# The S5 layer and the last feed-forward pass of a two-layer streaming encoder, computed in token halves and woven into dense passes

## The chip, the cores and the metric

The kernel runs on 1 core of one Trainium2 chip. The metric is the device time of one execution in microseconds (us), lower is better. Three runs of the kernel before stand beside one profiled execution, from which every row below is read.

## The reference

The model has two layers and works on 1024 prompt tokens and 64 sample tokens at once (T = 1088), D_MODEL = 1024, hidden width 2816. All tensors are float32. Layer 0 (a projection, stick-breaking attention beside a gated mixer, an output projection) and its SwiGLU feed-forward are the same before and after. Layer 1 is an S5 state-space mixer, a GLU and a SwiGLU feed-forward; the part that matters is, cut:

```python
def swiglu(h, w_gate, w_up, w_down):
    return (jax.nn.silu(h @ w_gate) * (h @ w_up)) @ w_down

def s5_mixer(h, h0_re, h0_im, ...):
    x_re = einsum('gpc,blgc->blgp', bb_re, ug)         # 64 groups of 16 channels, 64 complex states each
    x_im = einsum('gpc,blgc->blgp', bb_im, ug)
    ...                                                # first step also takes in the given state
    _, _, s_re, s_im = associative_scan(s[t] = a * s[t-1] + x[t])
    y = einsum('gcp,blgp->blgc', c_re, s_re) - einsum('gcp,blgp->blgc', c_im, s_im) + d_skip * u
    gl = gelu(y) @ w_glu
    ga, gb = split(gl, 2)
    return ga * sigmoid(gb), s_re[:, -1], s_im[:, -1]
```

Every layer is x = x + mixer(rmsnorm(x)), x = x + swiglu(rmsnorm(x)); a last rmsnorm follows.

## The kernel before, in words

**Dense matmuls.** Float32 products are made from three fp32r matmuls: every weight slab of 128 x 1024 is split into whi and wlo (slab_hi on ACT, slab_lo on POOL), every activation tile likewise into a high and a low part, and `three` (lines 248 to 253) issues wh*rh, wh*rl, wl*rh into one PSUM accumulation. All of these have a weight tile of 128 x 128.

**Stages.** (1) The input projection in three token chunks (384, 384, 320), with the tables of the S5 layer made beside it. (2) The "mid" stage: attention, output projection and feed-forward of layer 0, in two token halves (512 and 576 tokens, the second in two chunks of 288). It is planned in Python as a list of slots; each slot has dense groups (one PSUM bank each, three banks in turn) and, in some, attention steps, norm tiles or squares. Each engine walks through the same list. Attention of the second half is done beside the feed-forward of the first. (3) S5 (`s5_sp`, `s5_pe`, `s5_act`, `s5_dve`, `s5_pool`), for eight feature tiles f one after the other, over all 1088 tokens as 136 blocks of 8 steps. (4) The GLU (`glu_pe`) and (5) the norm and the feed-forward of layer 1 (`ffn_pe`, a loop of 10 passes and two halves around it), in the three token chunks 384, 384, 320. (6) The last norm, transposes and stores (`out_pe`).

**S5 in detail.** For each f TensorE does: 8 transposes of B (line 1830), 16 matmuls for a 16-row kernel table kt (line 1838, weight tiles 64 x 16), 16 input matmuls x (line 1850, weight tiles 128 x 64, two side by side), then 24 output matmuls y: 8 with the Toeplitz table tm (line 1868, weight tiles 128 x 128) and 16 with the state (line 1870, weight tiles 64 x 128). They are plain float32, and each such matmul stands in the trace as two records. Between x and y VectorE rotates, scans and rotates back (lines 1932 to 1984); the reordering of u, tm and y between partitions goes through DRAM by DMAs that SyncE issues. TensorE issues one f's x, then the y of the f before.

**Order.** Each engine works its own instructions in the written order and waits on semaphores; a wait holds up all that is behind it on that engine. The S5 stage begins when both halves of layer 0 are done, and the GLU needs gelu(y) of all eight f.

## Time and profile before

| | |
|---|---|
| median of 3 runs | 2809.38 us (2804.43 to 2810.51) |
| profiled execution | 2812.7 us, span 2810.9 us |
| mean granted TensorE clock | 0.941 |
| PE busy | 2565.4 us (91%) |
| DVE, ACT, POOL busy | 1166.2, 881.3, 1104.3 us |

The span runs from the first to the last instruction. Engines: PE is TensorE's matmuls, PEld its weight loads, DVE is VectorE, ACT ScalarE, POOL GpSimd, SP SyncE. A granted clock of 1.0 is TensorE's 2.4 GHz, 0.5 its 1.2 GHz. A record's duration overlaps with its neighbours', so the pace of TensorE is read from the distance of two starts, not from durations.

### The profile page before, as it was taken

The page shows a single profiled execution, that of the slowest core. Times are in us where ns is not written, and L with a number is a line of the kernel's source. Part 1 is how long each engine was busy: PE and PEld are TensorE (multiplying, and loading weights), DVE is VectorE, ACT ScalarE, POOL GpSimd, SP SyncE. Part 2 cuts the span into 40 slices and gives each one's busy share as a digit, 9 for nine tenths or more (in the row PEclk, how much of TensorE's full clock was granted, in tenths as well). Part 3 has the DMA queues.
Part 4 walks back from the last instruction along what each step waited for, and adds up shares of the span by engine and source line. Part 5 has one row for each costly group of instructions (what it writes and reads, how often), then busy time and mean ns, then how long its engine had stood idle before and what let it go on. Part 6 is the DMA issues. An engine that isn't in the chain of part 4 may idle for free.

```text
span 2810.9 us, 38283 instructions
## 1 busy us (share of the span) xinstructions
PE 2565.4 (91%) x15274; PEld 2364.7 (84%) x15274; DVE 1166.2 (41%) x1877; ACT 881.3 (31%) x1304; POOL 1104.3 (39%) x770
## 2 busy tenths in 40 slices
PE   6998949899997999999999587799699999999998
PEld 4898936677776978999999466799699999999998
DVE  3696637765562232422223677322412222222224
ACT  3423236788882322211221121311311111111114
POOL 2545534564454565544444200333532222222223
PEclk9999969899998999999999677899899999999999
DMA  4315664323423223322222675311011111111111
GB/s 121 103 59 198 243 200 115 86 72 82 110 72 123 83 83 98 106 83 90 76 84 68 170 195 149 126 46 46 29 40 44 41 42 44 45 45 45 45 45 64
DMA packets 290436, 254.11 MB, mean 90 GB/s; under 512 B 32561, under 2 KB 254705, under 8 KB 289025
## 3 DMA queue, kind: packets, MB, share of 16 engines
q1 hardware_dynamic: 282064, 219.96, 27.3%
q0 software_dynamic: 7088, 31.15, 2.9%
q8 instruction: 91, 1.49, 0.2%
q10 hardware_dynamic: 1152, 1.18, 0.1%
q14 instruction: 41, 0.33, 0.0%
HBM read 195.08 MB, written 54.80 MB: 89 GB/s over the span
## 4 chain that ended last, share of the span: by engine, by line
PE 75%; DVE 9%; DMA 5%; POOL 4%; ACT 2%; issue 2%; SPq 1%; POOLq 0%; DVEq 0%; ACTq 0%
PE ps L251 22%; PE ps L252 22%; PE ps L253 22%; PE ps L982 3%; PE ps L1870 1%; PE ps L994 1%; DVE v L1932 1%; DMA mst<-mT 1%; DVE fbuf L423 1%; PE ps L1868 1%; POOL hlo L431 1%; PE ps L974 1%; DVE t L1707 1%; POOL ssum L349 1%; PE ps L970 1%
## 5 line engine op out<-in xcount | busy, mean ns | idle before, releaser
L245 POOL TENSOR_TENSOR wlo<-raw,whi 128x1024 fp32r<-128x1024 f32 x250 | 602.8, 2420 | 402.1 <-ACT whi L241 400.4
L251 PE MATMUL ps<-hhi,whi 128*128 128x384 f32 (+1 forms) x1920 | 635.8, 331 | 49.0 <-POOL hlo L2019 14.9
L252 PE MATMUL ps<-hlo,whi 128*128 128x384 f32 (+1 forms) x1920 | 631.3, 329 | 0.0
L253 PE MATMUL ps<-hhi,wlo 128*128 128x384 f32 (+1 forms) x1920 | 631.1, 329 | 0.0
L251 PEld LDWEIGHTS ps<-hhi,whi 128*128 128x128 f32 x1920 | 365.2, 190 | 54.8 <-issue 22.5
L252 PEld LDWEIGHTS ps<-hlo,whi 128*128 128x128 f32 x1920 | 365.3, 190 | 0.3 <-issue 0.2
L253 PEld LDWEIGHTS ps<-hhi,wlo 128*128 128x128 f32 x1920 | 364.9, 190 | 0.0
L241 ACT ACTIVATE whi<-raw 128x1024 fp32r<-128x1024 f32 x250 | 259.1, 1054 | 312.9 <-PE ps L253 145.6
L251 PE MATMUL ps<-hB,whi 128*128 128x288 f32 x832 | 247.3, 297 | 12.3 <-POOL lB L1316 12.3
L509 POOL TENSOR_TENSOR gl<-fbuf,gh 128x384 f32 (+3 forms) x66 | 63.9, 968 | 488.8 <-DVE gh L564 488.8
L253 PE MATMUL ps<-hB,wlo 128*128 128x288 f32 x832 | 246.4, 296 | 0.0
L252 PE MATMUL ps<-lB,whi 128*128 128x288 f32 x832 | 246.2, 296 | 0.0
L561 DVE TENSOR_TENSOR fbuf<-ps,abuf 128x384 f32<-128x384 f32 (+1 forms) x66 | 35.4, 536 | 452.5 <-ACT abuf L479 448.2
L479 ACT ACTIVATE abuf<-ps 128x384 f32<-128x384 f32 (+1 forms) x66 | 31.1, 473 | 559.8 <-PE ps L253 559.8
L251 PE MATMUL ps<-rh,whi 128*128 128x288 f32 (+1 forms) x528 | 177.4, 336 | 14.7 <-DVE xA L1364 6.4
L572 DVE TENSOR_TENSOR x<-ps,x 128x384 f32<-128x384 f32 (+1 forms) x264 | 141.3, 535 | 109.9 <-PE ps L253 108.7
L1354 DVE TENSOR_TENSOR fb<-ps,ab 128x288 f32<-128x288 f32 (+1 forms) x66 | 35.3, 536 | 365.2 <-PE ps L253 342.2
L252 PE MATMUL ps<-rl,whi 128*128 128x288 f32 (+1 forms) x528 | 175.0, 332 | 0.0
L253 PE MATMUL ps<-rh,wlo 128*128 128x288 f32 (+1 forms) x528 | 174.8, 331 | 0.0
L253 PE MATMUL ps<-gh,wlo 128*128 (+2 forms) x528 | 172.1, 326 | 0.0
L252 PE MATMUL ps<-gl,whi 128*128 (+2 forms) x528 | 172.0, 326 | 0.0
L251 PE MATMUL ps<-gh,whi 128*128 (+2 forms) x528 | 172.0, 326 | 0.0
(315 smaller groups left out, 4796.6 us busy)
## 6 DMA issues: line engine op xcount, KB each, us to landing
raw<-in_ffn_w_gate SPq DMA_DIRECT2D x66, 512.0 KB, 3.8
raw<-in_ffn_w_up SPq DMA_DIRECT2D x66, 512.0 KB, 3.9
raw<-in_ffn_w_down SPq DMA_DIRECT2D x66, 512.0 KB, 3.6
raw<-in_ab_w_in SPq DMA_DIRECT2D x20, 512.0 KB, 4.1
raw<-in_ab_w_out SPq DMA_DIRECT2D x16, 512.0 KB, 3.8
raw<-in_ssm_w_glu SPq DMA_DIRECT2D x16, 512.0 KB, 3.9
dC<-co POOLq DMA_DIRECT2D x4, 1152.0 KB, 4.7
ca<-dC SPq DMA_DIRECT2D x8, 576.0 KB, 4.9
```

What stands on the lines that cost most here:

```text
L241: act.activation(whi[:, slot(t), :], raw[:, t % 2, :], ACT.Copy).then_inc(sem("w_hi"), 1)
L245: pool.tensor_tensor(wlo[:, slot(t), :], raw[:, t % 2, :], whi[:, slot(t), :].bitcast(F32), ALU.subtract).then_inc(sem("w_lo"), 1)
L251: pe.matmul(out, wh, rh, start=first, stop=False)
L252: pe.matmul(out, wh, rl, start=False, stop=False)
L253: return pe.matmul(out, wl, rh, start=False, stop=last)
L349: pool.tensor_tensor(ssum[:, c, 0:n], ssum[:, c, 0:n], sqbuf(k, a)[:, 0:n], ALU.add).then_inc(sem("n_add"), 1)
L479: act.activation(abuf[:, v % 2, 0:n], ps[:, 2 * (v % 2), 0:n], ACT.Silu).then_inc(sem("pair_act"), 1)
L509: pool.tensor_tensor(gl[:, bass.ds(o, n)], fbuf[:, v % 2, 0:n], gh[:, bass.ds(o, n)].bitcast(F32), ALU.subtract).then_inc(sem("hid_lo"), 1)
L561: dve.tensor_tensor(fbuf[:, v % 2, 0:n], ps[:, 2 * (v % 2) + 1, 0:n], abuf[:, v % 2, 0:n], ALU.mult).then_inc(sem("pair_used"), 1)
L572: dve.tensor_tensor(xo, acc(v)[:, 0:n], xo, ALU.add).then_inc(sem("acc_used"), 1)
L982: mm = pe.matmul(out, mat[:], r, start=mat is tri and u["first"] and j == 0, stop=True, skip_group_check=True)
L1354: dve.tensor_tensor(fb2[:, h % 2, 0:n], out, ab2[:, h % 2, 0:n], ALU.mult).then_inc(sem("use_v"), 1)
```

## The change

The whole of layer 1 moves into the slot list, in token halves of 512 (64 blocks of 8) and 576 (72 blocks); the second half's chunks become 256 and 320. There are now four feed-forward passes in a row: layer 0 half A, layer 0 half B, layer 1 half A, layer 1 half B. The S5 of half A is done in the pass of layer 0 half B, the S5 of half B in the pass of layer 1 half A; F runs from 0 to 15 over both. The GLU of a half is put ahead of the last down projection of the pass in which its S5 was done. The weights of layer 1's GLU and feed-forward are loaded and split once for each half, as those of layer 0 already were; the loop of `ffn_pe` goes.

The transposes of B and the kernel tables (`pre_pe`) are made once, in the pass of layer 0 half A, after attention, and kept in DRAM for both halves. The input matmuls `s5_x_pe` and the output matmuls `s5_y_pe` are made twice as often, with 64 or 72 moving columns where there were 136. All three are generators: `three` takes one step of them after each dense matmul that doesn't close a group. For each F the input matmuls stand in a gate slot, the scan (`s5_scan`, DVE) two slots later, the output matmuls five slots later, in the second down slot of the part.

VectorE's scan waits for its own instructions less often than before. The state at the end of half A is carried to half B. The last norm, transposes and stores of half A are put into the pass of layer 1 half B, and only those of half B come at the end.

```diff
-HCH = [[(0, 512)], [(512, 288), (800, 288)]]
+HCH = [[(0, 512)], [(512, 256), (768, 320)]]
...
-        def three(pe, out, s, col, rh, rl, first, last):
+        def three(pe, out, s, col, rh, rl, first, last, side=iter(())):
 
             wh, wl = whi[:, s, col:col + P], wlo[:, s, col:col + P]
             pe.matmul(out, wh, rh, start=first, stop=False)
+            next(side, None)
             pe.matmul(out, wh, rl, start=False, stop=False)
-            return pe.matmul(out, wl, rh, start=False, stop=last)
+            next(side, None)
+            mm = pe.matmul(out, wl, rh, start=False, stop=last)
+            if not last:
+                next(side, None)
+            return mm
 
...
+        def glu_slots(half, m):
+            chunks = range(len(HCH[half]))
+            tb = slab(w_glu[:, :, D + m * P:D + (m + 1) * P])
+            ta = slab(w_glu[:, :, m * P:(m + 1) * P])
+            yield [group("sig", half, c, m, [tb]) for c in chunks]
+            yield [group("lin", half, c, m, [ta]) for c in chunks]
...
+        passes = [(0, 0), (0, 1), (1, 0), (1, 1)]
+
+        def sequence():
+            for no, (layer, half) in enumerate(passes):
+                if no != 1:
+                    yield "pair", layer, half, 0
+                for i in range(PARTS):
+                    yield "pair", layer, half, 2 * i + 1
+                    if i + 1 < PARTS:
+                        yield "pair", layer, half, 2 * i + 2
+                    elif no == 0:
+                        yield ("pair", *passes[1], 0)
+                    yield "down", layer, half, i
...
+                    rms_slot(k, h)
+                    end = norm_soon(k, h, 1, 8 if (k, h) == (3, 1) else 4)
+                    if k == 2:
+                        soon(end - 1, hs=[h])
+                        soon(end, sl=[8 * h], st=[8 * h])
+                        stage["f"][h], stage["free"][h] = 0, len(SLOTS) + end + 1
...
+        for kind, layer, half, n in sequence():
+            if kind == "pair" and (layer, half, n) == (0, 1, 0):
+                assert stage["mix"] == -1 and not stage["rms"]
+            if kind == "down" and n == PARTS - 1 and (layer, half) in ((0, 1), (1, 0)):
+                h = layer
+                while stage["glu"][h] is None or stage["glu"][h] >= len(SLOTS):
+                    new_slot()
+                if stage["glu"][h] >= 0:
+                    run_glu(h)
             make = pair_slots if kind == "pair" else down_slots
-            for gs in make(half, n):
-                last = squares(gs, (2, half)) if kind == "down" and n == PARTS - 1 else []
-                new_slot(gs, sq=last, **hooks())
-                if mixer_b[0] == 1:
-                    mixer_b[0] = 2
-                    rms_slot(1)
-                    q1, q2 = tiles_of(1), tiles_of(2)
-                    todo.extend([dict(nt=q1[0:4]), dict(nt=q1[4:8]), dict(nt=q2[0:4]), dict(nt=q2[4:8])])
-                if norm2 == 1 and not todo:
-                    norm2 = 2
-                    rms_slot(0)
-                    todo.extend([dict(nt=tiles_of(3)[2 * k:2 * k + 2]) for k in range(4)])
-            if mixer_b[0] == 0 and not todo:
-                mixer_b[0] = 1
+            for b, gs in enumerate(make(layer, half, n)):
+                work = {}
+                gate = G[gs[0]]["kind"] == "gate"
+                if (layer, half) == (0, 0):
+                    work["at"] = some_steps()
+                if kind == "down" and n == PARTS - 1:
+                    work["sq"] = squares(gs, 2 if layer == 0 else 4, half)
+                for h in range(2):
+                    f = stage["f"][h]
+                    if gate and n % 2 and f is not None and f < KD and len(SLOTS) >= stage["free"][h]:
+                        F = 8 * h + f
+                        work["sx"] = [F]
+                        stage["f"][h], stage["free"][h] = f + 1, len(SLOTS) + 5
+                new_slot(gs, **work)
+                for F in work.get("sx", []):
+                    soon(2, sc=[F])
+                    if F % KD < KD - 1:
+                        soon(4, sl=[F + 1])
+                    soon(5, sy=[F])
+                    soon(6, sv=[F])
+                    if F % KD < KD - 1:
+                        soon(6, st=[F + 1])
+                    soon(7, so=[F])
+                    soon(8, sz=[F])
+                    soon(9, sg=[F])
...
+        def side_pe(pe, S):
+
+            for f in S["pre"]:
+                yield from pre_pe(pe, f)
+            for F in S["sx"]:
+                yield from s5_x_pe(pe, F)
+            for F in S["sy"]:
+                yield from s5_y_pe(pe, F)
...
-                mm = three(pe, out, slot(t), col, r1, r2, j == 0, j == count - 1)
+                mm = three(pe, out, slot(t), col, r1, r2, j == 0, j == count - 1, side)
...
+                side = side_pe(pe, S)
                 for n, g in enumerate(gs):
                     if at and len(gs) == 1:
-                        dense_pe(pe, g, lambda: at_pe_rest(pe, at[-1]))
+                        dense_pe(pe, g, side, lambda: at_pe_rest(pe, at[-1]))
                         continue
                     if at and n == len(gs) // 2:
                         at_pe_rest(pe, at[-1])
-                    dense_pe(pe, g)
+                    dense_pe(pe, g, side)
...
+        def pre_pe(pe, f):
+
+            pe.wait_ge(sem(f"br_in{f % 2}"), 16 * (f // 2 + 1))
+            if f:
+                pe.wait_ge(sem("e_BT"), 2 * f)
+                pe.wait_ge(sem("e_K"), 2 * f)
+            else:
+                pe.wait_ge(sem("u_c"), NU)
+                pe.wait_ge(sem("u_t"), NU)
+            for q in range(8):
+                mm = pe.transpose(ps[:, 3 + q // 4, (q % 4) * P:(q % 4 + 1) * P], br[f % 2][:, q // 2, q % 2, :], ident[:])
+                if q < 7:
+                    yield
+            mm.then_inc(sem("s_B"), 1)
+            yield
+            pe.wait_ge(sem("cp_in"), 16 * (f + 1))
+            for g in range(8):
+                j, a = divmod(g, 2)
+                r = slice(64 * a, 64 * a + 64)
+                for q in range(2):
+                    mm = pe.matmul(ps[0:16, 5 + a, j * P:(j + 1) * P], br[f % 2][r, j, q, P - 16:P], cp[r, j, q, 0:P],
+                                   start=q == 0, stop=q == 1)
+                if g < 7:
+                    yield
+            mm.then_inc(sem("s_K"), 1)
+
+        def pre_act(act, f):
...
+        def s5_x_pe(pe, F):
+            h, f = divmod(F, KD)
+            nn = NN[h]
+            pe.wait_ge(sem("bt_in"), 16 * (F + 1))
+            pe.wait_ge(sem(f"u_in{F % 2}"), 16 * L * (F // 2 + 1))
+            if F:
+                pe.wait_ge(sem("e_X"), banks_of(F - 1))
+            else:
+                pe.wait_ge(sem("e_BT"), 2 * KD)
+            for q in range(2):
+                for j in range(4):
+                    o = (4 * q + j) * nn if h == 0 else j * nn
+                    for a in range(2):
+                        mm = pe.matmul(ps[64 * a:64 * a + 64, 3 + (q if h else 0), o:o + nn],
+                                       bt[h][:, j, q, 64 * a:64 * a + 64], u[h][:, F % 2, 2 * j + a, :], start=True, stop=True,
+                                       skip_group_check=True)
+                    if (q, j) != (1, 3):
+                        yield
+            mm.then_inc(sem("s_X"), 1)
...
+        def s5_y_pe(pe, F):
+            h, f = divmod(F, KD)
+            nn = NN[h]
+            pe.wait_ge(sem("tm_in"), 16 * (F + 1))
+            pe.wait_ge(sem("ca_in"), 16 * (F + 1))
+            pe.wait_ge(sem("s_sh"), F + 1)
+            if F:
+                pe.wait_ge(sem("e_Y"), 2 * F)
+            else:
+                pe.wait_ge(sem("e_K"), 2 * KD)
+            for g in range(8):
+                j, a = divmod(g, 2)
+                r = slice(64 * a, 64 * a + 64)
+                out = ps[:, 5 + a, j * nn:(j + 1) * nn]
+                pe.matmul(out, tm[h][:, g, :], u[h][:, F % 2, g, :], start=True, stop=False)
+                yield
+                for q in range(2):
+                    mm = pe.matmul(out, ca[h][r, j, q, :], sh[h][r, q, j, :], start=False, stop=q == 1)
+                    if g < 7 or q == 0:
+                        yield
+            mm.then_inc(sem("s_Y"), 1)
+
...
-            s5_pe(pe)
-            glu_pe(pe)
-            pe.wait_ge(sem("glu_res"), NC * KD)
-            ffn_pe(pe, F1)
-            out_pe(pe)
```

## Rows read from the trace of the kernel before

**Rows 1.** Page: busy us (share) of each engine, and the chain by engine.
```profile
PE 2565.4 (91%) x15274; PEld 2364.7 (84%) x15274; DVE 1166.2 (41%) x1877; ACT 881.3 (31%) x1304; POOL 1104.3 (39%) x770
...
PE 75%; DVE 9%; DMA 5%; POOL 4%; ACT 2%; issue 2%; SPq 1%; POOLq 0%; DVEq 0%; ACTq 0%
```

**Rows 2.** Windows: start:end, length, busy (records) per engine, clock, DMA share, GB/s.
```profile
1180.00:1553.00 373.00, 373.00 (x2815) 373.00 (x2816) 104.21 (x242) 78.04 (x108) 172.62 (x105) 1.00 0.26 77
1553.00:1780.00 227.00, 155.17 (x970) 116.56 (x969) 151.57 (x277) 44.75 (x93) 14.78 (x17) 0.68 0.63 167
...
1974.00:2023.00 49.00, 28.06 (x117) 24.05 (x118) 29.97 (x31) 19.08 (x34) 30.89 (x31) 0.79 0.05 15
2023.00:2789.00 766.00, 764.72 (x4655) 764.63 (x4653) 197.11 (x392) 114.91 (x175) 228.75 (x148) 1.00 0.14 42
2789.00:2811.00 22.00, 11.41 (x78) 10.07 (x78) 6.97 (x11) 7.44 (x12) 0.54 (x1) 0.84 0.53 203
```

**Rows 3.** Timeline, PE, dense matmuls: start us, duration, line, weight tile, moving shape.
```profile
774.52 0.28 PE L982 MATMUL ps<-sphi,tri 128*128 128x256 f32 x1
774.63 0.28 PE L982 MATMUL ps<-splo,tri 128*128 128x256 f32 x1
...
1800.06 0.31 PE L253 MATMUL ps<-hhi,wlo 128*128 128x320 f32 x1
1800.20 0.31 PE L251 MATMUL ps<-hhi,whi 128*128 128x320 f32 x1
...
1989.05 0.33 PE L253 MATMUL ps<-hhi,wlo 128*128 128x384 f32 x1
1989.23 0.33 PE L251 MATMUL ps<-hhi,whi 128*128 128x384 f32 x1
```

**Rows 4.** The same, PE: short matmuls of another weight tile between dense ones.
```profile
847.13 0.28 PE L982 MATMUL ps<-sphi,tri 128*128 128x64 f32 x1
847.24 0.28 PE L982 MATMUL ps<-splo,tri 128*128 128x64 f32 x1
847.45 0.34 PE L994 MATMUL ps<-tz,vv 128*64 128x64 f32 x4
847.71 0.50 PE L251 MATMUL ps<-rh,whi 128*128 128x512 f32 x1
848.05 0.40 PE L252 MATMUL ps<-rl,whi 128*128 128x512 f32 x1
848.28 0.39 PE L253 MATMUL ps<-rh,wlo 128*128 128x512 f32 x1
```

**Rows 5.** The same, PE and PEld: S5's output matmuls, at either clock.
```profile
1690.82 0.47 PE L1868 MATMUL ps<-u,tm 128*128 128x136 f32 x2 [0.16 <-DVE kt L1946]
1691.22 0.73 PE L1870 MATMUL ps<-sh,ca 64*128 64x136 f32 x4
1691.88 0.50 PE L1868 MATMUL ps<-u,tm 128*128 128x136 f32 x2
...
1691.22 0.53 PEld L1870 LDWEIGHTS ps<-sh,ca 64*128 64x128 f32 x4
...
1603.48 0.79 PE L1868 MATMUL ps<-u,tm 128*128 128x136 f32 x2 [3.85 <-DVE kt L1946]
1604.20 1.27 PE L1870 MATMUL ps<-sh,ca 64*128 64x136 f32 x4
1605.40 0.82 PE L1868 MATMUL ps<-u,tm 128*128 128x136 f32 x2
```

**Rows 6.** Window of one f's output matmuls; columns as in rows 2.
```profile
1749.00:1764.00 15.00, 15.00 (x48) 11.21 (x48) 3.64 (x2) 0.00 (x0) 0.00 (x0) 0.50 0.11 37
```

**Rows 7.** Lines, DVE in S5, by shape: busy us, mean ns | idle before.
```profile
L1932 DVE TENSOR_TENSOR v<-xx,e 128x544 f32<-128x544 f32 x32 | 23.2, 725 | 1.1
```

**Rows 8.** Chain of waits in the third norm: start us, us, what.
```profile
1983.00 1.35 DVE fbuf L423
...
1986.01 1.35 DVE fbuf L423
```

More of the change, by code:

```diff
@@ L1067, in down_slots @@
-        def down_slots(half, i):
-            ts = [slab(w_down[0][(2 * i + j) * P:(2 * i + j + 1) * P, :]) for j in range(2)]
+            tg = slab(w_gate[layer][:, :, n * P:(n + 1) * P])
+            tu = slab(w_up[layer][:, :, n * P:(n + 1) * P])
+            yield [group("gate", half, c, n, [tg], layer) for c in chunks]
+            yield [group("up", half, c, n, [tu], layer) for c in chunks]
+        def glu_slots(half, m):
[4 more added lines that the diff above has]
+            yield [group("lin", half, c, m, [ta]) for c in chunks]
@@ L1069, in down_slots @@
+        def down_slots(layer, half, i):
+            ts = [slab(w_down[layer][(2 * i + j) * P:(2 * i + j + 1) * P, :]) for j in range(2)]
             if half == 0:
                 for b in range(2):
-                    yield [group("down", 0, 0, m, ts) for m in range(4 * b, 4 * b + 4)]
+                    yield [group("down", 0, 0, m, ts, layer) for m in range(4 * b, 4 * b + 4)]
             else:
                 for c in range(2):
-                    yield [group("down", 1, c, m, ts) for m in range(KD)]
+                    yield [group("down", 1, c, m, ts, layer) for m in range(KD)]
@@ L1076, in build, with rms_slot, norm_soon @@
+        def rms_slot(k, half):
+            gs = [group("rms", half, c, 0, []) for c in range(len(HCH[half]))]
+            new_slot(gs)
+        def norm_soon(k, half, first, per):
+            tl = tiles_of(k, half, per)
+            for i, v in enumerate(tl):
+                soon(first + i, nt=v)
+            return first + len(tl)
         new_slot(at=some_steps(), ms=[0, 1])
@@ L1160, in build @@
-        rms_slot(1)
-        new_slot(nt=tiles_of(4), out=[1])
-        new_slot(nt=tiles_of(5))
-        NG = len(G)
-        rms_group = [g for g in range(NG) if G[g]["kind"] == "rms"]
-        assert len(rms_group) == len(NORMS) and IN_TILES + len(SRC) == SLAB_GLU and step_no[0] > NU
-        last_group, last_slot = {}, {}
+                tb = slab(w_out[:, :, m * P:(m + 1) * P])
+                gs = [group("outB", 1, c, m, [tb]) for c in range(2)]
+                new_slot(gs, sq=squares(gs, 1, 1))
@@ new lines, in build @@
+        new_slot(os=[1])
+        for tt in range(4, 9):
+            new_slot(ot=[tt], oo=[tt])
+        assert not later and not stage["rms"] and stage["glu"] == [-1, -1], (later, stage)
+        NG = len(G)
+        NSLAB = IN_TILES + len(SRC)
+        rms_of = {NORMS.index((k, h, c)): None for k, h, c in NORMS if k < 4}
+        for q, g in zip([q for q in sorted(rms_of, key=lambda q: q)], [g for g in range(NG) if G[g]["kind"] == "rms"]):
+            rms_of[q] = g
+        q_of = {g: q for q, g in rms_of.items()}
@@ L1170, in build @@
                 last_group[t], last_slot[t] = g, G[g]["slot"]
[L1171 to L1174 removed]
+                first_slot.setdefault(t, G[g]["slot"])
+                first_group.setdefault(t, g)
         t = IN_TILES + 2
@@ L1222, in x_load @@
             sp.dma_start(x_half[half], xs3[:, :, s:s + n]).then_inc(sem(f"x_in{half}"), 16)
-        def x_store(sp, half):
-            s, n = HALF[half]
-            used(sp, max(g for g in range(NG) if G[g]["kind"] == "down" and G[g]["half"] == half))
-            sp.dma_start(xs3[:, :, s:s + n], x_half[half]).then_inc(sem("x_out"), 16)
         def mid_sp(sp, ahead):
```

1301 lines of the change are left out of this document (562 added, 739 removed).

## The prediction

> **What bounds the kernel now.** I read the page first: TensorE is busy 91% of the span, holds 75% of the chain that ended last, and no other engine is busy over 42% [rows 1]. So time goes only where TensorE gets less to do, runs slower, or stands still, and the change has to be priced in TensorE's time. The windows then say where it is not dense [rows 2]. Layer 0's half B takes 373 us for 2815 matmuls and layer 1's feed-forward 766 us for 4655, that is 0.1325 and 0.1646 us each at a granted clock of 1.00: nothing to gain there. Three stretches behind layer 0 are different. S5 holds up the dense work for 227 us (clock 0.68). The norm ahead of the last feed-forward is 49 us long; its 117 records are some 111 dense matmuls, worth 19 us at 0.17 us each, so 30 us are lost. The last norm and the stores take 22 us. Together 279 us, 10% of the span, and this is what the change can take away.
>
> **The dense matmuls** change only their widths. Distances of two starts give their pace: 0.11 to 0.12 us for 256 columns, 0.147 for 320, 0.17 to 0.18 for 384 [rows 3], and 0.23 for 512 [rows 4]. A weight tile met 384 + 384 + 320 columns in layer 1 (0.173 + 0.173 + 0.147 = 0.493 us) and meets 512 + 256 + 320 (0.227 + 0.120 + 0.147 = 0.494). In layer 0's half B, 0.267 stand where 2 x 0.1325 = 0.265 stood, 1584 times. Sum: +4 us. The second load and split of layer 1's weights costs nothing: layer 0's half B does the same for as many slabs per us with TensorE at 100% [rows 2]; were that cover gone, TensorE would wait for slabs, which those rows don't show.
>
> **The short matmuls put one by one** are the heart. `three` takes one step of a generator after a dense matmul, and most steps have another shape of weight tile than the dense 128 x 128. The trace has such a place: attention's four records with 128 x 64 tiles and 64 columns between two 128 x 128 ones [rows 4]. The matmul ahead of them has 0.21 us to itself where the pace of its kind is 0.11; the four take 0.26 (847.45 to 847.71); the dense one behind takes 0.34 where the next, of the same kind, takes 0.23. So one visit costs 0.10 + 0.26 + 0.11 = 0.47 us. Both ends of it are overhead: something of 0.10 us is waited out when the tile shape changes, and the first weight load in the new shape (0.11) stands in the open. The S5 stage shows the same at its own switches [rows 5]: four 64 x 128 records take 0.66 us from start to start, 0.11 for the exposed load, 0.09 for the way back, and about 0.115 each.
>
> The Trainium skill weighs the other way in "TensorE: Matmul & The Clock Gate", section "Step-by-step: what each phase is for": weight loads are pulled ahead of matmuls in flight where row groups don't conflict or the background weights are free. By that a visit would cost little more than its own records, and the S5 sum below would be some 140 us. The skill also has the opposite rule, in "TensorEngine Tiling (Array Packing)", section "Key Properties": a change of tiling mode drains TensorE. Rows 4 and 5 side with the second.
>
> Now the visits.
> - Input matmuls x: 8 visits of four 128 x 64 records for each F, 16 F: 128 x 0.47 = 60 us.
> - y, state part: 16 visits for each F, each one plain float32 matmul (two records) with a 64 x 128 tile. Its price from the same pieces: 0.10 to leave, 0.11 + 0.11 for its two weight loads (the second longer than the 0.05 us of 64 columns, so it isn't hidden), 0.05 for the last columns, 0.09 back, 0.11 for the dense load: 0.57 us. 256 x 0.57 = 146 us. Bounds: 0.35, if a load of half the rows is quicker, and 0.66, the whole four-record block.
> - y, Toeplitz part: same tile shape as dense, so no switch; two records at 0.11 each. 128 x 0.22 = 28 us.
> - The tables, once: 64 transposes at 0.11 = 7 us, and 64 visits of four records in one 64 x 16 tile, 0.10 + 4 x 0.11 + 0.09 + 0.11 = 0.74 us (bounds 0.5 and 0.9): 47 us.
> - In half A's down slots only 20 steps find a place and four of the 24 follow in a block: -3 us.
>
> Sum 285 us, where the same matmuls in blocks, without switches between, would be about 140. So the visits alone eat the 279 us.
>
> **Clock.** With 320-column neighbours three visits of y (two state, one Toeplitz) and their three dense matmuls last 3 x 0.147 + 2 x 0.57 + 0.22 = 1.80 us, most of it switches and exposed loads. The output matmuls of before are the nearest thing: they too pay loads and switches in the open, and at least in this window they ran at 0.50 throughout [rows 6], 1.92 us for a block of tm and state (1603.48 to 1605.40, [rows 5]) against 1.06 at full clock (1690.82 to 1691.88). The dense stages never fell [rows 2]. I take the clock to fall in part of y's stretches in half B: each is 24 x 0.147 + 16 x 0.57 + 8 x 0.22 = 14.4 us, of which some 9 would run 1.8 times as long, plus 3 for the dense matmuls behind; 10 us each, in 8 stretches 80. Bounds: 0, and 230 if all of the 285 us ran at the lower level.
>
> **Norms and ends.** Norms stay on the path where they fall into a slot: DVE works the eight tiles between evictions, and TensorE has three banks to run ahead. From the third norm, two tiles of 384 take 3.0 us [rows 8], so 1.5 each, 1.9 for 512. Half A's split norm: 8 x 1.9 = 15 us plus the sum and the root, of which the down groups hide a part; 20 lost. Half B's: 15. S5's own norm in half B, which DVE did in the open, is spread over four slots: 8. Three waits for a last square and its sum, 3 each: 9. At the end 5 output tiles stand where 9 stood: 14 of the 22 stay, and 4 are added for half A's. Sum 70 us, bounds 45 and 110.
>
> **Other queues.** The scan puts some 18 tensor operations on DVE in one go ahead of a slot's evictions. They took 0.73 us for 544 elements [rows 7], so 0.35 for 256 and about 8 us per F; it stands in the gate slots, where the next bank that DVE must free is needed 9 us later, so I cost it at nothing (1 to 2 us per F if that slips, 30 in all). SyncE gets some 21 short DMAs for each F between the slab loads; a part lasts 33 us and more, so it keeps up. If a wait inside a generator is late, all dense matmuls behind it on TensorE wait too.
>
> **The sum**, against the profiled execution's span: 2811 - 279 + 4 + 285 + 80 + 70 = 2971 us. The run is 2 us longer than its span, and 3 us above the median: 2970.
>
> **Rivals.**
> - *The switches are hidden* (the change does what its form suggests). Loads run ahead under 512 or 320 columns, S5 costs 140 us and the clock stays up: 2811 - 279 + 4 + 140 + 70 = 2746, faster. For it: where tile shapes agree, loads hide fully (0.11 us for 64 columns, rows 4). Against: neither switch of rows 4 nor those of rows 5 is hidden, not even the way back into 512 columns. It decides at a visit's price: below about 0.3 us on average over the 448 switching visits the change gains.
> - *The clock stays up.* Switches as priced, no fall: 2890. For it: one f of before did its output matmuls at the higher level [rows 5]. Against: rows 6.
> - *The clock falls in both halves and around x and the tables too*: 230 in place of 80, 3120. For it: TensorE's windows of S5 at 0.68 [rows 2]. Against: beside 512 columns the dense part of a stretch is longer.
> - *A generator's wait comes late.* A table, u or the scan is not there when its first step is taken; TensorE stands still for 4 us in each of 16 F: 3035. Against: five slots, over 25 us, lie between x and y, where before scan and transfers took less.
>
> **Chances.** The forecast's own case 0.47, clock stays up 0.20, falls everywhere 0.12, late waits 0.07, switches hidden 0.14. Under 0.2%, 6 us, a measurement can't tell this kernel from no change; nearly nothing lies there. Faster 0.14, same 0.02, slower 0.84. The range leaves out the hidden case and the far end: 2850 to 3120.
>
> **What would show it.** At a step inside a gate group: dense starts 0.32 to 0.34 us apart around four 128 x 64 records, right; 0.23, wrong. Input matmuls about 9 us per half-A gate slot where 5.4 is the dense part. Output slots of half B 17 us at full clock and near 27 at the lower. The granted clock in the pass of layer 0 half B well under 1.00, and in the pass of layer 1 half A nearer to it; layer 1 half B at 0.16 us for each dense matmul, as before. No hole of 227 us. If a visit's price is under 0.3 us, or the clock is 1.00 in all passes and the norms are hidden, the forecast is wrong.

## The result: 7.3% slower

| | before | after |
|---|---|---|
| median (fastest to slowest) | 2809.95 us (2804.43 to 2812.79, 4 runs) | 3018.36 us (2999.15 to 3019.26, 4 runs) |
| span of the profiled execution | 2810.9 us | 3017.5 us |
| mean granted TensorE clock | 0.941 | 0.923 |

The ratio is 1.0728, 95% interval 1.0682 to 1.0774. The forecast was 2970 us (2850 to 3120), 48 us below the median. First the page of the kernel after: TensorE's row, its granted clock in 40 slices, and the chain by engine.

```profile
PE 2805.0 (93%) x15914; PEld 2411.2 (80%) x15914; DVE 1241.7 (41%) x2098; ACT 904.1 (30%) x1331; POOL 1320.0 (44%) x848
...
PEclk7998979899997999987888799998899999999999
...
PE 74%; DVE 14%; DMA 4%; POOL 4%; issue 2%; ACT 1%; SPq 1%; DVEq 0%; POOLq 0%; ACTq 0%
```

TensorE's share of the span is higher than in [rows 1], its busy time grew by 240 us, and its clock is down in the slices from 1280 to 1740 us, where half A's S5 is woven into the pass of layer 0 half B. A busy share of 93% says nothing of how dense the work is. Next the windows (start:end, length, busy and records of PE, PEld, DVE, ACT, POOL, clock, DMA share, GB/s). The first three are whole stages: layer 0 half B with S5, layer 1 half A with S5, and layer 1 half B without it. The next four are single strips, one slot's visits with the dense matmuls between and beside them. From here on "half A" and "half B" of a strip name the pass in which it stands, and so its neighbours: 512 columns in layer 1 half A, 256 or 320 in layer 0 half B. The S5 done in a pass is that of the other token half.

```profile
1240.00:1750.00 510.00, 505.66 (x3020) 445.91 (x3020) 187.49 (x409) 70.66 (x105) 146.46 (x81) 0.84 0.31 90
1960.00:2395.00 435.00, 416.12 (x1838) 303.76 (x1839) 178.25 (x368) 69.27 (x97) 141.43 (x65) 0.93 0.39 111
2650.00:3000.00 350.00, 350.00 (x2627) 350.00 (x2626) 105.10 (x230) 76.99 (x113) 163.60 (x99) 1.00 0.26 78
...
1247.22:1251.97 4.75, 4.75 (x43) 3.15 (x42) 0.49 (x1) 1.06 (x1) 2.35 (x1) 1.00 0.02 5
1282.67:1303.66 20.99, 20.99 (x79) 15.72 (x78) 2.39 (x5) 0.00 (x0) 1.57 (x1) 0.66 0.37 100
2003.00:2019.31 16.31, 16.31 (x75) 10.91 (x74) 3.46 (x5) 1.39 (x3) 4.06 (x3) 1.00 0.51 134
955.88:964.67 8.79, 8.79 (x59) 5.80 (x58) 0.49 (x1) 1.42 (x2) 3.22 (x2) 1.00 0.68 191
```

Layer 1 half B, without visits, still gives 0.133 us a matmul at a clock of 1.00, like the first window of [rows 2]. The two stages with S5 don't. A strip's own cost is its length less its dense matmuls at the pace of [rows 3, 4]; I call that its extra. The first strip is x in half B: 4.75 - 9 x 0.120 = 3.67 us for 8 visits, 0.46 each. The third is y in half A at full clock: 16.31 - 25 x 0.227 = 10.63 us. The fourth is a strip of `pre_pe`, the tables: 8.79 - 17 x 0.120 = 6.75 us. The second is y in half B: 20.99 - 29 x 0.147 = 16.7 us, and its clock is 0.66. How one visit looks, in the timeline of TensorE, beside the attention visit of [rows 4]:

```profile
1247.22 0.28 PE L252 MATMUL ps<-hB,whi 128*128 128x256 f32 x1
1247.43 0.34 PE L1569 MATMUL ps<-u,bt 128*64 128x64 f32 x4
1247.70 0.38 PE L254 MATMUL ps<-lB,whi 128*128 128x256 f32 x1
1248.01 0.34 PE L1569 MATMUL ps<-u,bt 128*64 128x64 f32 x4
```

From one visit to the next it is 0.58 us for 0.120 us of dense work. The dense matmul between them has 0.31 us to itself: the load that nothing covers, its columns, and the wait when the tile shape changes again.

Last, what TensorE waited for (engine, line, releaser: us, times, longest), in 860 to 1240 us (the load of B for the tables, and the low part of a weight slab) and in 1960 to 2395 us (VectorE's eviction of an up group, which stands behind the scan):

```profile
PE ps L1462 <- DMA br<-dB: 19.0, 2, 11.9
PE ps L252 <- POOL wlo L246: 9.5, 3, 5.3
```

```profile
PE ps L252 <- DVE fb L1268: 18.1, 8, 2.3
```

### The profile page after: what moved, and what is told of

It is laid out like the page before. It is cut to its first block, busy times and chain, and to the rows that moved or that the text cites. A ratio compares the mean times of both kernels' runs of the same rounds, so it can differ in the third digit from the quotient of the medians.

```text
span 3017.5 us, 39380 instructions
## 1 busy us (share of the span) xinstructions
PE 2805.0 (93%) x15914; PEld 2411.2 (80%) x15914; DVE 1241.7 (41%) x2098; ACT 904.1 (30%) x1331; POOL 1320.0 (44%) x848
## 4 chain that ended last, share of the span: by engine, by line
PE 74%; DVE 14%; DMA 4%; POOL 4%; issue 2%; ACT 1%; SPq 1%; DVEq 0%; POOLq 0%; ACTq 0%
PE ps L252 20%; PE ps L254 20%; PE ps L256 20%; PE ps L1593 4%; PE ps L751 2%; DVE vw L1660 2%; PE ps L763 1%; PE ps L1569 1%; PE ps L1472 1%; DMA mst<-mT 1%; PE ps L1590 1%; DVE xx L1677 1%; DVE fb L1268 1%; DVE xx L1660 1%; POOL wlo L246 1%
## 5 line engine op out<-in xcount | busy, mean ns | idle before, releaser
L252 PE MATMUL ps<-hB,whi 128*128 128x320 f32 (+1 forms) x1792 | 539.2, 301 | 9.0 <-POOL lB L1255 4.1
L254 PE MATMUL ps<-lB,whi 128*128 128x320 f32 (+1 forms) x1792 | 538.7, 301 | 0.0
L256 PE MATMUL ps<-hB,wlo 128*128 128x320 f32 (+1 forms) x1792 | 538.2, 300 | 0.0
L1268 DVE TENSOR_TENSOR fb<-ps,ab 128x512 f32<-128x512 f32 (+2 forms) x156 | 83.5, 535 | 872.2 <-PE ps L256 795.6
L252 PE MATMUL ps<-rh,whi 128*128 128x512 f32 (+2 forms) x1056 | 384.0, 364 | 54.2 <-DVE fb L1268 18.1
L254 PE MATMUL ps<-rl,whi 128*128 128x512 f32 (+2 forms) x1056 | 387.6, 367 | 0.0
L256 PE MATMUL ps<-rh,wlo 128*128 128x512 f32 (+2 forms) x1056 | 385.4, 365 | 0.0
L252 PE MATMUL ps<-hA,whi 128*128 128x512 f32 x896 | 364.5, 407 | 8.3 <-POOL wlo L246 4.2
L254 PE MATMUL ps<-lA,whi 128*128 128x512 f32 x896 | 359.1, 401 | 0.0
L256 PE MATMUL ps<-hA,wlo 128*128 128x512 f32 x896 | 358.7, 400 | 0.0
L254 PEld LDWEIGHTS ps<-lB,whi 128*128 128x128 f32 x1792 | 343.7, 192 | 4.6 <-issue 2.7
```

The source lines that it names most:

```text
L252: pe.matmul(out, wh, rh, start=first, stop=False)
L254: pe.matmul(out, wh, rl, start=False, stop=False)
L256: mm = pe.matmul(out, wl, rh, start=False, stop=last)
L1268: dve.tensor_tensor(fb2[:, h % 2, 0:n], out, ab2[:, h % 2, 0:n], ALU.mult).then_inc(sem("use_v"), 1)
```

## The experiments

The theory was that of the prediction: a visit's cost is the change of tile shape on the way in and out with a weight load in the open each way, and the clock falls behind many such visits. The rivals: the records themselves cost this wherever they stand; or late tables and transfers do it. Twelve kernels were run, each against the kernel before. Where two are compared below, it is by these ratios.

| run | median us | ratio to before (95%) | extra x / tables / y, us | at clock 0.5, 860 to 2700 us |
|---|---|---|---|---|
| after | 3018.4 | 1.0728 (1.0682 to 1.0774) | 71 / 79 / 227 | 314 |
| all in blocks | 2866.8 | 1.0203 (1.0179 to 1.0226) | 21 / 29 / 164 | 239 |
| y in blocks | 3004.9 | 1.0687 (1.0659 to 1.0715) | 110 / 78 / 166 | 403 |
| state with 128 rows | 2842.9 | 1.0117 (1.0093 to 1.0141) | 61 / 75 / 87 | 99 |
| blocks, y in sweeps | 2737.2 | 0.9738 (0.9713 to 0.9762) | 21 / 29 / 62 | 82 |
| before, y in sweeps | 2784.4 | 0.9923 (0.9901 to 0.9944) | | |
| sweeps, tables one by one | 2781.2 | 0.9920 (0.9898 to 0.9943) | 21 / 73 / 62 | 92 |
| sweeps, x one by one | 2785.2 | 0.9928 (0.9909 to 0.9948) | 66 / 31 / 65 | 102 |
| sweeps, y one by one | 2914.7 | 1.0391 (1.0358 to 1.0424) | 21 / 28 / 215 | 273 |
| sweeps by half | 2748.6 | 0.9797 (0.9769 to 0.9824) | 21 / 30 / 72 | 75 |
| y spaced | 2981.2 | 1.0628 (1.0598 to 1.0657) | 98 / 73 / 165 | 263 |
| state in pairs | 2890.0 | 1.0288 (1.0260 to 1.0316) | 61 / 73 / 139 | 113 |
| sweeps, scan cut in two | 2863.4 | 1.0195 (1.0170 to 1.0219) | 21 / 29 / 62 | 208 |

The extras are sums over all 16 strips of x, 8 of the tables and 16 of y, by the rule above, from the records of each profiled execution; a wait for a late table or a lower clock inside a strip is in them. The last column adds up the stretches that the trace marks at a granted clock of 0.5.

**All in blocks (e1).** The steps are no longer taken in `three`; the loop that empties the generators behind the slot's last group runs them in one go.

```diff
             pe.matmul(out, wh, rh, start=first, stop=False)
-            next(side, None)
             pe.matmul(out, wh, rl, start=False, stop=False)
-            next(side, None)
-            mm = pe.matmul(out, wl, rh, start=False, stop=last)
-            if not last:
-                next(side, None)
-            return mm
+            return pe.matmul(out, wl, rh, start=False, stop=last)
```

> The changed kernel with every generator run in one go behind the slot's last dense group; the same instructions, slots and halves. Theory (the price is the coming and going of each visit): the visits cost 427 us one by one; in blocks 16 x 2.2 us for x, 16 x 7 to 8.5 us for y (0.88 to 1.06 us for a group of Toeplitz and state matmuls) and about 40 us for the tables, some 200 us, and the clock stays up in the dense part: 2790 us, 2840 if the clock falls inside the blocks. Rival (the records themselves cost this wherever they stand, or S5's place in the passes does): within 1% of 3018 us.

2867 us: 0.0525 of the time of before, 148 us, is won, and the rival "wherever they stand" is out. But the theory promised 2790 to 2840. The windows of a block of x, of tables and of two of y:

```profile
1208.27:1209.35 1.08, 1.08 (x33) 1.01 (x32) 0.00 (x0) 0.97 (x2) 0.00 (x0) 1.00 0.03 11
948.68:951.51 2.83, 2.83 (x41) 2.39 (x40) 0.57 (x2) 2.39 (x4) 1.91 (x2) 1.00 0.38 112
...
1241.87:1252.42 10.55, 10.55 (x50) 9.01 (x48) 0.49 (x1) 1.06 (x1) 2.34 (x1) 0.66 0.34 105
1502.79:1511.93 9.14, 9.14 (x50) 7.80 (x49) 0.49 (x1) 1.06 (x1) 2.34 (x1) 0.79 0.39 118
```

A strip's extra for x fell from 3.67 or 3.9 us to 1.3, for the tables from 6.75 to 2.9 (the windows leave out the way in and out). y did not get dense: within a block it still changes its tile shape for each of eight groups (Toeplitz, state, Toeplitz, ...), 9.1 to 10.9 us a block where the expectation had 7 to 8.5, and the clock falls inside each. That is the missed part.

**y in blocks (e2).** As after, but y is kept back and run behind the slot's groups.

```diff
             for F in S["sy"]:
-                yield from s5_y_pe(pe, F)
+                held.append(s5_y_pe(pe, F))
...
                 for _ in side:
                     pass
+                for part in held:
+                    for _ in part:
+                        pass
+                held.clear()
```

> Only the output generator y runs in one go behind the slot's groups; x and the tables stay one by one. Theory: y one by one costs 256 x 0.65 + 128 x 0.3 = 205 us at the full clock and nearly all of the 80 us of lower clock, in a block 125 us: 2860 us, and the stretches at the lower clock beside y of half B are gone. Rival (the lower clock comes from something else, as S5's transfers or the scan): about 2940 us, with the lower clock still there.

A clear miss: 3005 us, 0.4% under after (its interval ends at 1.0715, after's starts at 1.0682, so the two aren't told apart). The lower clock is not gone but longer, 403 us against 314. The windows of a y block and of the x strip right behind it:

```profile
1289.16:1299.66 10.50, 10.50 (x51) 8.97 (x49) 0.49 (x1) 1.06 (x1) 2.34 (x1) 0.66 0.34 102
1300.17:1307.07 6.90, 6.90 (x41) 4.39 (x40) 0.00 (x0) 0.25 (x1) 0.00 (x0) 0.50 0.53 152
```

The block takes 10.5 us in place of a strip's 15.9 to 18.9 us of extra, 60 us won in all, but it ends in the next slot's x visits, and those (14 strips of 16) now run at 0.50 from end to end: x's extra is 110 us in place of 71. With one visit per dense matmul on one side and a block full of changes on the other, nothing dense stands between.

**State with 128 rows (e3).** Both operands of the state matmul take all their rows. Its y is then not the reference's; only its time is read here.

```diff
-                    mm = pe.matmul(out, ca[h][r, j, q, :], sh[h][r, q, j, :], start=False, stop=q == 1)
+                    mm = pe.matmul(out, ca[h][:, j, q, :], sh[h][:, q, j, :], start=False, stop=q == 1)
```

> The changed kernel, but each state matmul uses all 128 rows of its two operands in place of 64 (so S5's output is left wrong): same number of instructions at the same places, but with the tile shape of the dense matmuls. Theory (the change of tile shape is what is paid): a state visit falls from 0.65 to about 0.3 us, as the Toeplitz ones, 256 x 0.35 = 90 us less, 2930 us, and down to 2850 if the clock then stays up too. Rival (the price is the plain float32 operands or the small number of columns, not the shape): within 0.5% of 3018 us.

2843 us: 172 us less (0.0611), for the same number of instructions in the same places with the same columns. This is the strongest single piece: it is neither plain float32, nor short columns, nor the interleaving as such; it is the change of tile shape. The y strip answering to the second of after:

```profile
1281.66:1291.26 9.60, 9.60 (x79) 9.60 (x78) 2.39 (x5) 0.00 (x0) 1.58 (x1) 1.00 0.82 218
```

5.34 us of extra for 24 visits, 0.22 each, PEld busy throughout and the clock at 1.00. In half A's strips it is 5.54 in place of 10.63, so the shape costs 5.1 / 16 = 0.32 us a visit; 256 of them are 82 us. The other 90 us are mainly clock: 99 us at 0.5 where there were 314, and 215 us at the 0.42 us lost for each, which is worked out further down, are 90.

**Blocks, y in sweeps (e4).** Inside a block the eight Toeplitz matmuls come first, then the sixteen of the state with upper and lower rows in turn.

```diff
             for g in range(8):
                 j, a = divmod(g, 2)
-                r = slice(64 * a, 64 * a + 64)
-                out = ps[:, 5 + a, j * nn:(j + 1) * nn]
-                pe.matmul(out, tm[h][:, g, :], u[h][:, F % 2, g, :], start=True, stop=False)
+                pe.matmul(ps[:, 5 + a, j * nn:(j + 1) * nn], tm[h][:, g, :], u[h][:, F % 2, g, :], start=True, stop=False, ...)
                 yield
-                for q in range(2):
-                    mm = pe.matmul(out, ca[h][r, j, q, :], sh[h][r, q, j, :], start=False, stop=q == 1)
+            for q in range(2):
+                for g in range(8):
+                    ...
+                    mm = pe.matmul(ps[:, 5 + a, ...], ca[h][r, j, q, :], sh[h][r, q, j, :], start=False, stop=q == 1, ...)
```

> As the kernel with all generators in blocks, and y in two sweeps: the eight Toeplitz matmuls first, then the sixteen state matmuls (alternating between upper and lower rows), so that a block changes its tile shape twice in place of sixteen times. Theory: 7 changes less each way, 0.2 to 0.3 us each, 16 F: 20 to 35 us less than the plain blocks, about 2760 us. Rival (a change costs nothing inside a block of short matmuls): equal to the plain blocks within 0.3%.

2737 us, 131 us under the plain blocks, four times what I expected, and 2.6% faster than the kernel before. Its windows of a y block in half B and in half A:

```profile
1242.29:1246.05 3.76, 3.76 (x51) 3.62 (x49) 0.49 (x1) 1.06 (x1) 2.35 (x1) 1.00 0.54 152
1821.05:1824.82 3.77, 3.77 (x50) 3.62 (x48) 0.69 (x1) 1.06 (x1) 2.34 (x1) 1.00 0.93 205
```

3.76 us where it was 9.1 to 10.9. So y's extra went from 164 to 62 us, and neither in the 16 blocks nor right behind them does the clock fall. TensorE spent 157 us less at 0.5 than in the plain blocks. The expectation had counted only the changes, not that the clock comes back and that neighbours on other rows overlap.

**Before, y in sweeps (e5).** The same order in S5 of the kernel before, nothing else.

> The kernel before, with nothing changed but the order inside S5's output block: the eight Toeplitz matmuls first, then the sixteen state matmuls, upper and lower rows in turn. It asks how much of the sweep's gain belongs to the change. Theory (TensorE bounds that stage): a group costs 1.06 us at the full clock and 1.92 at half; the sweep takes off some 0.45 us of each of 64, 29 us at the full clock and 50 at half, and the clock may come back: 2760 to 2780 us. Rival (the stage waits for the scan and its transfers): under 10 us, 2800 us or more.

2784 us, 22 us (0.8%) under before. The sweep is thus worth something without the change, and a fair price of moving layer 1 into halves, with S5 in blocks, is 0.9738 against 0.9923: 52 us won, not 74.

**One kind at a time (e6, e7, e8).** Each is the kernel with sweeps, with one generator taken one by one again.

> The kernel with blocks and the sweep (2737 us), and the tables' steps alone put one by one again. Theory, by the prices read in the changed kernel at the full clock (0.22 us a transpose, 0.85 us a visit of four 64 x 16 records) against 2.94 us for the block of 40 records: 8 x (8 x 0.22 + 8 x 0.85 - 2.94) = 45 us, 2782 us, some 10 more where the clock falls. Rival (prices of the prediction, 0.11 and 0.74): 31 us, 2768 us. Rival (what the changed kernel lost there, 70 us, comes from a late table or transfer): more than 60 us.

> The kernel with blocks and the sweep, and x alone one by one again. Theory by the price read in the changed kernel: 16 x (8 x 0.577 - 1.32) = 53 us, 2790 us, clock up. Rival (price of the prediction, 0.47): 39 us, 2776 us.

> The kernel with blocks and the sweep, and y alone one by one again (in the sweep's order: eight Toeplitz visits, then sixteen state visits, two neighbours on other rows). Theory: at the full clock 16 x (8 x 0.33 + 16 x 0.65 - 3.87) = 147 us, 2884 us; with the lower clock in each of the eight stretches of half B, some 75 us, 2960 us. Rival (the lower clock of the changed kernel needs the Toeplitz and state visits to alternate): 2884 us.

By the ratios they cost 51, 53 and 184 us; 288 together, where after stands 0.0990, 278 us, above the kernel with sweeps. So the three parts make up all of it. Tables and x hit my number, but for another reason than the one written down. The prices there (0.22 and 0.85, 0.577, 0.65 and 0.33 us) were read visit by visit, and are some 0.1 us too high each, because what stands between two visits belongs in part to the dense matmul: the 0.58 us above hold its 0.120. The strips tell it rightly: seven of the tables' strips at 6.85 us (the undisturbed ones cost 6.72 to 6.88) as against 2.94 in a block are 27 us, which is the prediction's price; the other 18 of the 45 us of extra are the wait for B's load and the clock behind it. So the late tables are a part of it after all. x costs 61 - 21 = 40 us at the full clock, again the prediction's price, 5 us more where the clock fell or TensorE waited (4 of them in one strip), and 8 lie outside the strips. y's strips would come to some 162 us at the full clock (9.5 in half A as three of them show, 10.8 in half B by taking away what the lower clock cost), 100 more than in blocks; with the lower clock they give 215 - 62 = 153. The rest of the 184, 31 us, fits the dense matmuls beside the strips: outside all strips the clock was at 0.5 for 60 us longer than in the kernel with sweeps, and there 320 columns take 0.267 us in place of 0.147. Two strips of y:

```profile
1232.90:1253.04 20.14, 20.14 (x80) 14.70 (x78) 2.39 (x5) 0.00 (x0) 1.58 (x1) 0.68 0.38 105
1972.15:1987.31 15.16, 15.16 (x74) 10.37 (x73) 3.46 (x5) 0.77 (x1) 3.71 (x2) 1.00 0.55 144
```

The first is beside 320 columns, the second beside 512; in half B the clock fell in eight strips of eight, in half A in five. So the alternation of Toeplitz and state isn't needed for the clock to fall beside short dense matmuls, and that rival is out.

**Sweeps by half (e9).** Four groups on the upper rows, then four on the lower: `for g in (0, 2, 4, 6, 1, 3, 5, 7)`.

> The kernel with blocks and the sweep, but the state matmuls of a sweep no longer alternate between the upper and lower 64 rows: four of one half, then four of the other. Same instructions, same two changes of tile shape. Theory: of the 3.4 us that the sweep took from a block, half is the pairing, in which two matmuls on different rows start 7 ns apart (32 records in 1.79 us, 0.056 each); without it they follow at 0.11, 1.7 us more for each of 16 blocks: 27 us, 2765 us. Rival (all of the gain is the changes of shape saved): 2737 us within 0.3%.

2749 us, 0.6% slower (the intervals, 0.9713 to 0.9762 and 0.9769 to 0.9824, just part). The block takes 4.35 us against 3.76, so 0.6 us hang on taking turns, not 1.7; in the records the two halves of the rows still overlap where one follows the other: the 32 state records take 2.53 us, 0.079 each, against 0.060 in turn and 0.11 for matmuls on the same rows.

```profile
1240.30:1244.65 4.35, 4.35 (x50) 4.22 (x48) 0.49 (x1) 1.06 (x1) 2.35 (x1) 1.00 0.47 132
```

How much of the sweep is changes saved and how much is overlap stays open: this run takes away only a part of the overlap.

**y spaced (e10).** An empty step behind each step of y, so that two or more dense matmuls stand between visits.

```diff
             for F in S["sy"]:
-                yield from s5_y_pe(pe, F)
+                for _ in s5_y_pe(pe, F):
+                    yield
+                    yield
```

> The changed kernel with an empty step behind each step of y: a visit after every second dense matmul of the slot, 20 of 24 find a place in half B's slots, 10 of 24 in half A's, the rest in a block behind. Theory (the clock falls by how much of a stretch TensorE spends in visits): half B's stretches stay up or nearly, 50 to 75 us less, and 14 steps in half A's block cost about 5 us less each time in place of 14 x 0.55, another 20 us: 2930 to 2950 us. Rival (any visits bring the clock down, and stretches twice as long are down twice as long): 3018 us or more.

2981 us, 28 us under after, less than expected. A y strip of half B and the x strip behind it:

```profile
1272.81:1290.38 17.57, 17.57 (x99) 13.69 (x98) 4.36 (x9) 1.27 (x2) 1.91 (x2) 1.00 0.47 120
1290.07:1296.97 6.90, 6.90 (x43) 4.55 (x42) 0.00 (x0) 0.66 (x2) 2.35 (x1) 0.61 0.50 173
```

The first half of the theory holds: spaced, y runs at 1.00 in all eight strips. The second doesn't: the strip now reaches up to the next x slot, and in five of the seven x strips that follow one the clock falls there, right behind. In half A, where 14 steps stay in a block full of changes, it falls in all seven x strips behind a y strip (x's extra 98 us for 71), and y itself saved next to nothing (9.2 to 10.9 us a strip for 10.6 to 10.9).

**State in pairs (e11).** The two state matmuls of a group make one step: 128 visits of four records in place of 256 of two.

```diff
                 for q in range(2):
                     mm = pe.matmul(out, ca[h][r, j, q, :], sh[h][r, q, j, :], start=False, stop=q == 1)
-                    if g < 7 or q == 0:
-                        yield
+                if g < 7:
+                    yield
```

> The changed kernel, but the two state matmuls of a group make one visit: 128 visits of four records in place of 256 of two, all else one by one as it was. Theory (a fixed price for coming and going, 0.43 us, and 0.11 for each record): 128 x (2 x 0.65 - 0.87) = 55 us less at the full clock and up to 25 more through the clock: 2940 to 2965 us. Rival (the price is in the records): 3018 us within 0.5%.

2890 us, 124 us less, more than the theory's 55 to 80. At the full clock a strip costs 8.0 to 8.2 us in place of 10.6 to 10.7, some 41 us in all and so less than the 55; the rest is clock. With it y costs 139 us in place of 227, and in six of eight strips of half B and all of half A the clock now stays at 1.00:

```profile
1391.09:1401.66 10.57, 10.57 (x69) 8.70 (x67) 1.90 (x4) 0.00 (x0) 1.20 (x1) 1.00 0.74 198
```

So the clock's part isn't proportional: taking away one of y's changes in two left 113 us at 0.5 where there were 314, and the kernel with sweeps has 82.

**Sweeps, scan cut in two (e12).** An attempt at the eight stops of TensorE behind VectorE's scan. `s5_scan` yields once, behind its two scan instructions, and what follows there is issued after the evictions of the next slot.

```diff
                 for F in S["sc"]:
-                    s5_scan(dve, F)
+                    half_done.append(s5_scan(dve, F))
+                    next(half_done[-1])
                 for g in gs[cut2:]:
                     evict_dve(dve, g)
+                if not S["sc"]:
+                    for scan in half_done:
+                        for _ in scan:
+                            pass
+                    half_done.clear()
```

> The kernel with blocks and the sweep, and VectorE's scan cut in two: its last part (four products, the sum and difference, the copies) is issued behind the next slot's evictions in place of ahead of them. Theory: the eight stops of TensorE of 2.65 us in layer 1's half A, each ended by VectorE's up eviction that stood behind the scan, go: 21 us less, 2716 us, 3.3% under the kernel before. Rival (the next wait is as late, for the last part then holds up the down evictions or y's own wait for the scan): within 5 us of 2737 us.

It went the other way by 128 us: 2863 us. What TensorE waited for in 1180 to 2500 us:

```profile
PE ps L252 <- DVE xA L1275: 75.2, 10, 8.1
PE ps L252 <- DVE xB L1275: 74.4, 10, 7.9
```

The stops of 2.3 us went, but the last part now stands ahead of the down projections' evictions. A down group is six matmuls, 0.7 us beside 256 columns and 1.4 beside 512, so three banks are soon full, and TensorE stood some 8 us in each of 16 F. Beside gate and up groups (24 matmuls, 2.9 to 5.4 us each) the same work was nearly hidden. The best kernel remains the one with blocks and sweeps, 2737 us.

## Why the prediction was right

Direction, mechanism and most sizes held; here step by step.

- **Removed, 279 us.** Layer 1 half B shows the dense stage without gaps; no stretch like the 227 us of [rows 2] is left. Nothing to correct.
- **Visits, 285 us.** At the full clock the strips give 283. x: 8 x 3.67 and, where no clock fell, 8 x 3.94 us: 61, forecast 60. Tables: five strips without a wait took 6.74 to 7.19 us (the last with 0.65 us at the lower clock); seven at 6.85, for two had a wait and a lower clock in them, and one block of 3.2: 51, forecast 54 (7 + 47). y: 10.63 us in half A. In half B no strip ran at the full clock; two with 12.3 and 19.6 us at the lower one took 20.1 and 23.2 us, which is 0.42 us lost for each at 0.5, and so 15.0 us without, 10.7 of extra. 8 x 10.63 + 8 x 10.7 = 171, forecast 146 + 28 - 3 = 171. The price of 0.57 for a state visit, put together from pieces of [rows 4, 5], was the number on which all hung; 10.7 us less eight Toeplitz visits at 0.22 leave 0.56 for each of sixteen. By the rule in the Trainium skill, "TensorE: Matmul & The Clock Gate", section "Step-by-step: what each phase is for" (loads are pulled ahead), they would have been half; the trace shows loads without a gap only while the tile shape stays, as in the run with 128 rows (PEld busy all 9.60 us). The rule of "TensorEngine Tiling (Array Packing)", section "Key Properties", that a change of mode drains TensorE, is the one that the trace agrees with: 0.32 us a visit hang on the shape.
- **Clock, 80 us.** It fell where forecast: in all eight y strips of half B and in no y strip of half A but for half a us. In those strips it cost 227 - 171 = 56 us; three x strips behind y in half A lost 10, the table strips 9. Together 75. Dense matmuls outside the strips come on top: 114 of 320 columns at 0.266 us in place of 0.147 in 1240 to 1750 us, and 83 of 512 at 0.424 in place of 0.227 in 1960 to 2395 us, 30 us. So the term was 105 us for 80, within its bounds; the forecast's own case had only the eight stretches of half B, which with the dense matmuls behind gave 70.
- **Scan at nothing.** Wrong by a size: 18 us, the row "DVE fb L1268" above, eight times 2.3 us. I had counted 8 us for the scan; in half B it took 12, hidden, and in half A 14 (1985.5 to 1999.4 us), for a reason given below. It stayed within the bound of 30.
- **A generator's wait comes late.** I gave it 64 us and 0.07, for x, y and scan. It came at the tables, 19 us, for the load of B from DRAM: the first steps of `pre` are taken at the start of the slot, and a wait there stops the dense work too. With the block at the slot's end the same wait was 2.6 us.
- **Norms and ends, 70 us.** 72 by the stretches around them (length less dense matmuls at their pace): 25 + 3 in 1855 to 1960 and 2395 to 2455 us, 27 in 2540 to 2630, 17 at the end.
- **Dense widths, +4 us.** The dense matmuls at their paces add up to 2086 us, before 2082.

Sum: 2811 - 279 + 4 + 283 + 105 + 18 + 19 + 72 = 3033, against a span of 3017.5. The 16 us too many are found ahead of layer 0's half B, where the sum has nothing but the tables: up to the 3500th dense matmul (1103 us before, 1165.5 after), what is neither dense nor a table strip is 435 us before and 418 after. No run asks why. The prediction's sum was low by 46 us: 18 for the scan, 19 for the tables' wait and 25 of clock, less these 17. That the faster front made up for part of the clock is luck; the price of the visits is not.

"Switches hidden" fell with the 0.46 and 0.56 us visits; "the clock stays up" with the eight strips; "falls everywhere" with layer 1 half A's y strips at 1.00. Most of the signs that the prediction named came true, the clock at 0.84 in the pass of layer 0 half B and 0.93 in that of layer 1 half A among them. Three of its readings were wrong. Layer 1 half B was to run at 0.16 us a dense matmul "as before"; 256 and 320 columns in turn are 0.1335 by its own paces, and 0.133 was measured. The hidden case decides not at 0.3 us a visit but, by its own terms with the clock up, at (279 - 4 - 70 - 28 - 7 + 3) / 448 = 0.39. And loads do not "hide fully" where the shape stays: 512 columns take 0.227 us, so 64 would take some 0.03 (an estimate), and the 0.11 us from start to start in [rows 4] are longer than that.

## What to carry to other kernels

Matmuls of another tile shape, put singly between dense ones, cost several times their own work: here 377 us where the same instructions cost 112 in blocks ordered by shape. Look first at how often the shape changes, and put the steps of one shape side by side before thinking about where they go; taking turns between upper and lower rows adds something on top. And work put on an evicting engine belongs into the slots whose banks are needed latest: the whole scan, 12 to 14 us of VectorE, cost nothing to 2.3 us ahead of an up group's eviction, and its last part alone, 8 us, cost some 8 ahead of the down groups'.

## What the runs showed of the hardware

**Clock.** It fell in and behind strips rich in changes of shape (48 records and 29 dense ones, clock 0.66), and equally inside a block without dense matmuls that changes its shape sixteen times (0.66). It stayed at 1.00 in a block of the same 48 records with two changes, and in a strip with the same 24 visits of the dense shape. It can come behind the work that brought it: spaced y ran at 1.00, and the x strip after it at 0.61.

**Tiles on different rows or columns.** 32 records of x, two tiles side by side, took 1.08 us in a block, 0.034 each, where 16 Toeplitz records at 128 x 128 follow each other at 0.11. The Trainium skill says in "TensorEngine Tiling (Array Packing)", section "Key Properties", that tiles load and multiply independently; these rows agree, though these weight tiles are also half as wide, and no run separates the two.

**VectorE held by GpSimd.** The scan's slowest instructions aren't its large ones. DVE and POOL in the kernel after:

```profile
1985.81 1.11 DVE L1677 TENSOR_TENSOR xx<-xx,p 128x4 f32<-128x4 f32 x1
...
1986.95 2.31 DVE L1677 TENSOR_TENSOR xx<-xx,p 128x4 f32<-128x4 f32 x1
...
1991.76 2.25 DVE L1660 TENSOR_TENSOR xx<-xx,carry 128x4 f32<-128x4 f32 x1
...
1993.93 0.15 DVE L1657 TENSOR_TENSOR xx<-xx,carry 128x4 f32<-128x4 f32 x1
```

```profile
1985.61 1.29 POOL L1238 TENSOR_TENSOR rl<-fb,rh 128x512 fp32r<-128x512 f32 x1 [2.71 <-DVE rh L1273]
1986.86 2.39 POOL L246 TENSOR_TENSOR wlo<-raw,whi 128x1024 fp32r<-128x1024 f32 x1
1991.39 2.60 POOL L246 TENSOR_TENSOR wlo<-raw,whi 128x1024 fp32r<-128x1024 f32 x1 [2.15 <-ACT whi L242]
```

Four elements a partition take 0.15 us, or 1.1 to 2.3 where they start beside a subtraction of GpSimd's, and then they end with it (1986.86 + 2.39 = 1989.25, and 1986.95 + 2.31 = 1989.26). The Trainium skill, "SBUF — State Buffer", section "Who interferes with whom", has this: a VectorE instruction with two inputs in SBUF waits for a GpSimd instruction that reads SBUF. The trace agrees, with 5.7 of the scan's 14 us in these three instructions. No run took the subtractions away, so this is read, not tested.
